# A hybrid encoder block on 8 cores: the opening pair made of both sequences' first groups, attention heads combined from PSUM, and the opening's loads and stages placed anew

## The chip, the cores and the metric

The kernel runs on the 8 NeuronCores of one Trainium2 chip. Each core takes 2 of the 16 sequences and the whole set of weights; the cores exchange nothing. The metric is the device time in microseconds of the slowest core, and the median of several runs.

## The reference, cut to what matters

Input and output are 16 sequences of 2048 tokens by 1024 floats. One layer:

```python
h = rms_norm(x);  proj = h @ w_in            # 1024 -> 2560: lru_x | lru_gate | q | k | v
lru_x = causal_dwconv(lru_x, width 4);  lru_h = rg_lru(lru_x)    # scan over time, 512 channels
out_a = gelu(lru_gate) * lru_h
p = softmax(q k^T / 8 + bias(T5) + block-causal mask)            # 4 heads, two maps per head
out_b = rms_norm((p1 - lam * p2) @ v)        # per head, value width 128
x = x + concat(out_a, out_b) @ w_out
h = rms_norm(x);  gate, val = split(h @ ffn_w_up)                # 2 x 3072
x = x + (gelu(causal_dwconv(gate, width 3)) * val) @ ffn_w_down
return rms_norm(x)
```

## The kernel before, in words

A core's 4096 tokens are cut into 8 groups of 512. `groups` (L642) lists them in the order of work: the four groups of sequence 0, then the four of sequence 1. Attention and the recurrence look back only, so group g of a sequence needs the keys, values and state of the groups before it; with g = 0 a head has 3 units of scores (two of 512 and one of 256 columns per map), with g = 1 it has 7, and 4 more for each further group.

The stages of a group are N (RMS norm and transposes), V, G, L, Q, K (the five 512-wide slabs of the input projection; L is the RG-LRU with its convolution, `lru` at L1005), B (attention, L1074), C (output projection, residual and second norm, L1181), and F or P (the MLP). The first two groups form a **pair** (`NP` = 2): they share each weight slab at the time when the weights come in as f32, are cast to bf16 and are written back to HBM (`load_slab`, `wslab`), and their residual rows stay in SBUF (`x0`). The MLP of the pair runs in thirds of its width (`stage_P`, L1250, with `plan` at L1415); later groups read the bf16 slabs back.

In B each head runs over its units: scores on TensorE (L1097), a bias on VectorE where the keys are near (L1114), exp on ScalarE (L1119), and the product with V on TensorE (L1130) into 8 regions of 129 columns in three PSUM banks, the last column being the sum of the weights. Three evictions (L901 on ScalarE, L903 on VectorE) then copy the regions to the SBUF tile `acp`, which frees the banks. Seven VectorE instructions follow: reciprocal (L1140), times -lambda (L1142), two products with the reciprocals (L1148, L1150), their sum (L1152), the square (L1153) and its row sum (L1155); then `rstd` (L849: an addition on VectorE at L850, a power on GpSimd at L853) and the product with it into `ob` (L1159).

No engine's order is written by hand. Each operation is a node with costs by engine and a priority; `schedule` (L162) places, node by node, the one that can start first by its estimated times, and among those that start together the one with the lowest priority number. That fixes the instruction order of every engine at build time, and on the chip each engine works in that order and waits on semaphores. The priorities come from `paced` (L1372), which spreads a stage over a stretch of "periods" from the tables `FR`, `PR`, `plan` and `e_` (L1387 to L1421). Where the estimate leaves TensorE idle, `_warm` (L306) puts in matmuls on a tile of zeros (L720). The four staging tiles for f32 weights lie in the key and value blocks of groups 2 and 3, so `claims` (L918) makes groups 2 and 3 wait until the staging is over.

At the start the SP queue issues the small parameters (L655), the f32 identity (L662, the first 128 columns of `stage`), then tiles of x (L651) and weights; the remaining 640 KB of `stage` come at L664. `ident` is cast on VectorE from the loaded one (L671), and the first transposes (L839) need it.

Of the kernel before, what the change touches and what calls it, by code (L numbers as in the profile page):

```python
# [9 lines left out]
F32 = mybir.dt.float32  # L10
BF16 = mybir.dt.bfloat16
# [10 lines left out]
SUBLN_EPS = 1e-5  # L22

# [56 lines left out]
class Node:  # L80
    __slots__ = ("i", "alts", "fn", "reads", "writes", "preds", "succs", "npred", "pri", "tab", "vts", "dma",
# [3 lines left out]
class Sched:  # L85
# [21 lines left out]
    def node(self, alts, fn, reads=(), writes=(), tab=None, dma=0, pri=None, tag="", after=(), behind=(), visit=None, soft=()):  # L107
        n = Node()
        n.i = len(self.nodes)
# [52 lines left out]
    def schedule(self, policy):  # L162
# [10 lines left out]
        dma_free = 0.0  # L173
# [35 lines left out]
        while placed < len(nodes):  # L209
            best = None  # L210
            for e in engs:
# [5 lines left out]
                for n in av:  # L217
# [50 lines left out]
            else:  # L268
                free[e] = t + hold
                n.fin = t + hold + TAIL[e]  # L270
# [178 lines left out]
def pack_params(inp):  # L449
# [31 lines left out]
    st.add("ident", np.eye(128, dtype=np.float32))  # L481
# [22 lines left out]
def build(nseq, S, pk_off, npar, nsmall, st_off, nst):  # L504
# [14 lines left out]
    wsl_d = nc.dram_tensor("wslab", [NSLAB, 128, 2048], BF16).ap()  # L519

    NPT, NSL = 3, 21

    with ExitStack() as st:
# [21 lines left out]
        lhalo = T("lhalo", [128, 4, 3], F32)  # L545
        lstate = T("lstate", [128, 4], F32)
        PT = T("PT", [128, NPT, 2, G], BF16)
        acp = T("acp", [128, 8, 129], F32)
# [3 lines left out]
        fhalo = T("fhalo", [128, 24, 2], F32)  # L552
# [10 lines left out]
        P_ob = Pool_("ob", 2)  # L563
        P_st = Pool_("stage", 4)
# [25 lines left out]
        for name, n in [("lam", 1), ("neglam", 1), ("e1", 1), ("e2", 1), ("s1", 1), ("s2", 1), ("cneg", 4), ("nba", 4),  # L590
                        ("nbx", 4), ("c2neg", 4), ("subg2", 1), ("mhalf", 1), ("rs", 8), ("rs2n", 4), ("sso", 4),
# [12 lines left out]
        b_stg2 = Buf()  # L604
        b_stage = [stg_vt, b_stg2]
        b_hT = [Buf() for t in range(NT)]
        b_hT2 = [Buf() for t in range(NT)]
        b_acp = Buf()
# [9 lines left out]
        b_lhaloc = [Buf() for c in range(4)]  # L618
        b_lstate = [Buf() for c in range(4)]
        b_fhalo = [Buf() for k in range(24)]  # L620
# [18 lines left out]

        S_.pri = 0  # L640
        ngrp = nseq * NG
        groups = [(sq, g) for sq in range(nseq) for g in range(NG)]  # L642
# [6 lines left out]
        def load_x(src_d, gi, t, cls, reads=(), **kw):  # L649
# [4 lines left out]

        node({"sp": 0.1}, lambda e: e.dma_start(out=prm[:, 0:nsmall], in_=par_d[:, 0:nsmall]), writes=[b_prm],  # L655
             dma=nsmall * 512, tag="prm", pri=-9)

        NP = 2
        x0 = [[load_x(x_d, 0, t, "XF", pri=-8 if t < 2 else -6.709) for t in range(NT)], []]
        stg_v = lambda: slot[:, stg_vt.s:stg_vt.s + 2, :].rearrange("p a b -> p (a b)")  # L660
        idn = Buf()
# [256 lines left out]
        def claims(gi):  # L918

            return {2: [b_stg], 3: [b_stg1]}.get(gi, [])  # L920
# [581 lines left out]
```

How the kernel before makes its waits and increments, by code:

```python
            def body(e):  # L403
                for fn, waits, sem, inc in self.prog[k]:
                    for s, v in waits:
                        e.wait_ge(self.sems[s], v)
                    if fn is not None:
                        fn(e).then_inc(self.sems[sem], inc)
```

The softmax here doesn't subtract the row's maximum and nothing guards it: scores larger than these inputs give would overflow.

## Time and profile before

| | us |
|---|---|
| median of 3 runs | 1764.8 (1762.7 to 1765.93) |
| span of the profiled execution, slowest core (core 0) | 1762.0 |
| span of core 1 in the same execution | 1754.9 |
| TensorE matmul busy on core 0, share of its span | 1694.3, 96% |
| VectorE, ScalarE, GpSimd busy on core 0 | 1168.4, 1072.0, 405.4 |

How to read it: the time of a run is that of its slowest core with some 3 us around the span. TensorE's busy time contains the matmuls on zeros, which do no work. Some of core 0's matmul records are missing from its trace (9445 matmuls beside 9628 weight loads), so the rows by stretch come from core 1, whose 9628 matmul records are whole.

### The profile page before, as it was taken

What the parts mean: (1) busy time and instruction counts of PE and PEld (TensorE: products, weight loads), DVE (VectorE), ACT (ScalarE), POOL (GpSimd) and SP (SyncE); (2) the same over time, 40 slices, a digit from 0 to 9 for tenths busy, and PEclk for the clock granted to TensorE, in tenths of its full rate; (3) what the DMA queues carried; (4) which work ended last, traced back from release to release, by engine and by line L of the source; (5) the groups of instructions that cost most, each with busy time, mean ns of one, the idle gap of its engine ahead of it and who ended that gap; (6) DMA issues with size and microseconds to landing.
All of it is one profiled execution on the core that took longest, in us unless ns stands there. A gap on an engine that the chain in (4) does not pass through costs nothing.

```text
span 1762.0 us, 31843 instructions; the slowest of 8 cores (1752.4 to 1762.0 us)
## 1 busy us (share of the span) xinstructions
PE 1694.3 (96%) x9445; PEld 803.9 (46%) x9628; DVE 1168.4 (66%) x2035; ACT 1072.0 (61%) x1419; POOL 405.4 (23%) x616
## 2 busy tenths in 40 slices
PE   8978899999999999999999999999999999999998
PEld 4434444444444444444444444444444444444443
DVE  3499857474687675757884597726877268764943
ACT  6778847356786586745854378444884458842721
POOL 2265413020331220113421042201322013210400
PEclk9999999999999999999999999999999999999999
DMA  9945299994447644559569545865458554447641
GB/s 275 293 142 170 69 304 290 290 289 144 147 155 239 191 153 137 190 161 268 187 207 266 149 172 203 230 203 171 147 171 223 189 169 147 161 140 218 223 175 72
DMA packets 165992, 340.53 MB, mean 193 GB/s; under 512 B 73664, under 2 KB 73920, under 8 KB 165696
## 3 DMA queue, kind: packets, MB, share of 16 engines
q1 hardware_dynamic: 165824, 338.49, 61.3%
q8 instruction: 81, 1.33, 0.3%
q14 instruction: 87, 0.71, 0.1%
HBM read 267.14 MB, written 55.57 MB: 183 GB/s over the span
## 4 chain that ended last, share of the span: by engine, by line
PE 83%; issue 5%; DVE 4%; DMA 4%; ACT 3%; POOL 1%; SPq 0%; DVEq 0%; ACTq 0%; POOLq 0%
PE pb L867 45%; PE pb L885 25%; PE pb L1130 6%; PE pb L1097 4%; DMA Va<-w_in 2%; PE pb L1328 1%; ACT PT L1119 1%; PE pb L720 1%; ACT raw L973 0%; DMA Va<-w_up 0%; DMA slot<-wslab 0%; DMA KT<-w_up 0%; DMA mixT<-ob 0%; ACT la L1031 0%; ACT thr L1031 0%
## 5 line engine op out<-in xcount | busy, mean ns | idle before, releaser
L867 PE MATMUL pb<-hT,slot 128*128 128x512 bf16 x3480 | 804.1, 380 | 18.1 <-issue 5.0
L867 PEld LDWEIGHTS pb<-hT,slot 128*128 128x128 bf16 x3584 | 336.0, 98 | 426.1 <-issue 52.3
L1119 ACT ACTIVATE PT<-pb,prm 128x1024 bf16<-128x1024 f32 (+1 forms) x288 | 305.7, 1063 | 153.3 <-PE pb L1097 74.0
L885 PE MATMUL pb<-slot,aT 128*128 128x512 bf16 x1494 | 345.0, 379 | 4.4 <-issue 1.4
L853 POOL TENSOR_TENSOR sm<-sm 128x1 f32<-128x1 f32 (+1 forms) x128 | 97.7, 765 | 633.4 <-DVE sm L850 633.1
L885 PEld LDWEIGHTS pb<-slot,aT 128*128 128x128 bf16 x1536 | 145.1, 98 | 178.7 <-issue 15.0
L1243 DVE TENSOR_TENSOR slot<-pb,slot 128x512 f32<-128x512 f32 x180 | 123.4, 688 | 142.5 <-PE pb L885 141.3
L1233 DVE TENSOR_TENSOR aT<-pb,aT 128x512 bf16<-128x512 f32 x192 | 130.6, 686 | 87.2 <-PE pb L867 82.4
L1130 PEld LDWEIGHTS pb<-Va,PT 128*128 128x128 bf16 x2176 | 142.5, 98 | 69.4 <-issue 20.6
L1130 PE MATMUL pb<-Va,PT 128*128 128x129 bf16 x2176 | 170.5, 221 | 2.0 <-ACT PT L1119 0.9
L990 DVE SCALAR_TENSOR_TENSOR facc<-raw,prm,facc 128x512 f32<-128x512 f32 x192 | 145.4, 761 | 32.1 <-ACT facc L984 22.7
L990 DVE SCALAR_TENSOR_TENSOR aT<-raw,prm,facc 128x512 bf16<-128x512 f32 x192 | 148.6, 778 | 7.3 <-DVE fhalo L976 0.3
L973 ACT ACTIVATE raw<-pb 128x512 f32<-128x512 f32 x164 | 97.7, 596 | 76.0 <-PE pb L867 51.4
L984 ACT ACTIVATE facc<-raw,prm 128x512 f32<-128x512 f32 x146 | 118.8, 814 | 27.6 <-DVE raw L973 9.8
L1114 DVE TENSOR_TENSOR pb<-pb,prm 128x512 f32<-128x512 f32 (+1 forms) x152 | 90.4, 595 | 49.4 <-PE pb L1097 47.9
L867 PE MATMUL pb<-aT,slot 128*128 128x512 bf16 x497 | 119.7, 384 | 3.4 <-DVE slot L904 2.2
L969 POOL COPY raw<-fhalo 128x2 f32<-128x2 f32 x168 | 68.0, 409 | 158.6 <-DVE aT L990 142.8
L885 PE MATMUL pb<-slot,mixT 128*128 128x512 bf16 x438 | 99.6, 382 | 2.6 <-DMA mixT<-ob 0.9
L1097 PE MATMUL pb<-qT,KT 64*128 64x512 bf16 (+3 forms) x576 | 98.3, 354 | 3.0 <-ACT PT L1119 2.7
L1224 ACT ACTIVATE aT<-aT 128x2048 bf16<-128x2048 bf16 x48 | 89.5, 1908 | 0.4 <-DVE aT L990 0.4
L814 ACT ACTIVATE hb<-slot 128x1024 bf16<-128x1024 f32 x38 | 40.0, 1053 | 69.5 <-DVE slot L1193 47.3
L1193 DVE TENSOR_TENSOR slot<-pb,slot 128x512 f32<-128x512 f32 x64 | 44.1, 689 | 55.1 <-PE pb L885 55.0
(138 smaller groups left out, 1662.9 us busy)
## 6 DMA issues: line engine op xcount, KB each, us to landing
slot<-wslab SPq DMA_DIRECT2D x326, 512.0 KB, 4.8
slot<-x SPq DMA_DIRECT2D x80, 512.0 KB, 7.1
wslab<-slot SPq DMA_DIRECT2D x50, 512.0 KB, 8.4
out<-slot SPq DMA_DIRECT2D x28, 512.0 KB, 5.5
x<-slot SPq DMA_DIRECT2D x24, 512.0 KB, 3.7
KT<-w_up SPq DMA_DIRECT2D x20, 512.0 KB, 6.4
Va<-w_up SPq DMA_DIRECT2D x20, 512.0 KB, 6.3
KT<-w_in SPq DMA_DIRECT2D x10, 512.0 KB, 10.6
```

The costliest lines, as they stand in the source:

```text
L853: op("pool", 1.0, lambda e: e.tensor_tensor(out=smv(rsn, 0, n), in0=smv(ssn, 0, n), in1=smv("mhalf").to_broadcast([128, n]), op=ALU.pow), ...
L867: last = e.matmul(bank(p), lhsT=w[:, kk, cc * 128:(cc + 1) * 128], rhs=src[:, hf * 4 + kk, :], start=(hf == 0 and kk == 0), stop=(hf == 1 ...
L885: last = e.matmul(bank(p), lhsT=src[:, k0 + hf * 4 + kk, t * 128:(t + 1) * 128], rhs=w[:, kk, :], start=(hf == 0 and kk == 0), stop=(hf == ...
L973: return e.activation(out=o, in_=bank(p), func=AF.Copy) if e is nc.scalar else e.tensor_copy(out=o, in_=bank(p))
L984: return e.activation(out=o, in_=i, func=AF.Identity, scale=w_ap[:, n:n + 1], bias=b_ap)
L990: nd = op("dve", dve_us(512, ptr=1), lambda e, k=k, last=last: e.scalar_tensor_tensor(out=out if last else tile[:, v.s, :], in0=raw[:, r_. ...
L1097: last = e.matmul(psum[:, s.s + c, n0:n0 + n], lhsT=KT[c * 64:(c + 1) * 64, j // NT, h, (j % NT) * 128:(j % NT + 1) * 128], rhs=q_()[c * 6 ...
L1114: op("dve", dve_us(2 * wn), lambda e, s=s, wn=wn, n0=n0, bias_ap=bias_ap: e.tensor_tensor(out=psum[:, s.s:s.s + 2, n0:n0 + wn], in0=psum[: ...
L1119: op("act", act_us(2 * N, ptr=1), lambda e, s=s, pt=pt, N=N, h=h: e.activation(out=PT[:, pt.s, :, 0:N], in_=psum[:, s.s:s.s + 2, 0:N], fun ...
L1130: last = e.matmul(psum[:, acc[ab].s, off:off + 129], lhsT=PT[:, pt.s, c, q0:q0 + 128], rhs=Va[:, j, h, 0:129], start=(j == 0 and rr % 3 == 0),
L1233: op("dve", dve_us(512), lambda e, p=p, a=a: e.tensor_tensor(out=aT[:, a, :], in0=bank(p), in1=aT[:, a, :], op=ALU.mult), reads=[p], write ...
L1243: return e.tensor_tensor(out=xs, in0=bank(p), in1=xs, op=ALU.add)
```

## The change

1. **Order of groups.** `groups` becomes (0,0), (1,0), (0,1), (0,2), (0,3), (1,1), (1,2), (1,3), written here as (sequence, group). The pair is now the first group of each sequence. Halos and states of the convolutions and the scan get one copy per sequence. Keys and values of (1,0) are kept in block 1, stored to a new HBM tensor `kv` (`save_v` and the end of `stage_K`, 0.5 MB each) and brought back into block 0 before group (1,1) (`bring_kv`). `claims` moves from groups 2 and 3 to 3 and 4.
2. **Heads combined from PSUM.** The 8 regions are laid out in three neighbouring banks held as one piece (class `acc`, first bank 2). The three evictions are gone. After reciprocal and -lambda, four 128-wide ScalarE instructions scale the second map from PSUM into the new `acp` tile, four 128-wide VectorE instructions multiply the first map from PSUM and add, four more square with an accumulated sum, and one 512-wide instruction applies `rstd` as before.
3. **Identity on chip.** A memset and an affine_select on GpSimd instead of load and cast.
4. **Opening loads.** The first x tile is issued first, then the small parameters, x tiles 1 to 3, the first weights, and only then `stage` in one piece.
5. **Estimates and places.** Costs of GpSimd operations are lowered; VectorE operations marked `lk` wait, in the estimate, for GpSimd to be free and keep it waiting until they end; the addition in `rstd` may go to GpSimd. All place tables have new numbers, and thirds 2 and 3 of `plan` change their order.

```diff
+PLAN = {
+    "PR": {"N0": (-6.075, -6.633), "N1": (-6.336, -5.832), "V": (-6.445, -6.616, 0.491), "G": (-6.224, -6.595, 0.644),
+           "L0": (-6.074, -5.643), "Q": (-5.988, -5.895, 0.207), "K": (-6.015, -5.702, 0.777), "L1": (-4.943, -3.721),
+           "B0": (-6.001, -5.45), "B1": (-4.798, -2.917), "C": (-4.561, -2.744)},
+    "P": [(-4.283, -3.284), (-3.436, -2.186), (0.46, 0.735), (-0.01, 0.432), (0.855, 2.235)],
+    "WB": 0.712,
+    "S": [-7.967, -6.709, -6.709, -6.3, -5.846],
+}
...
-        PR.update({'N0': (-6.391, -6.385), 'N1': (-6.336, -5.832), 'V': (-6.603, -6.546, 0.322), 'G': (-6.231, -6.583, 0.677), 'L0': (-6.098, -5.643), 'Q': (-5.988, -5.895, 0.497), 'K': (-6.015, -5.702, 0.672), 'L1': (-4.943, -3.721), 'B0': (-6.001, -5.45), 'B1': (-4.686, -3.5), 'C': (-4.573, -2.551)})
-        plan = [(0, {0: 0}, 'F', -4.391, -3.392), (1, {0: 0}, 'F', -3.299, -2.384), (0, {1: 8}, 'A', 0.124, 0.653), (1, {1: 0}, 'A', 0.66, 1.007), (2, {0: 8, 1: 0}, 'F', 0.855, 2.116)]
...
+                    if e == "dve" and n.lk:
+                        t = tt = max(t, free["pool"])
+                    elif e == "pool" and t < locked:
+                        t = tt = locked
...
-        groups = [(sq, g) for sq in range(nseq) for g in range(NG)]
+        groups = [(sq, 0) for sq in range(nseq)] + [(sq, g) for sq in range(nseq) for g in range(1, NG)]
+        kblock = lambda gi, i: gi if gi < NP else i
...
-        x0 = [[load_x(x_d, 0, t, "XF", pri=-8 if t < 2 else -6.709) for t in range(NT)], []]
-        node({"sp": 0.1}, lambda e: e.dma_start(out=stg_v()[:, 0:128], in_=stg_d[:, 0:128]), writes=[stg_vt, idn],
-             dma=128 * 512, tag="stg", pri=-8.5)
+        x0 = [[load_x(x_d, 0, t, "XF", pri=-20 if t == 0 else SP_[t - 1]) for t in range(NT)], []]
+        node({"sp": 0.1}, lambda e: e.dma_start(out=stg_v()[:, 0:nst], in_=stg_d[:, 0:nst]), writes=[stg_vt, b_stg2],
+             dma=nst * 512, tag="stg", pri=SP_[3], behind=[x0[0][0].ld])
+        op("pool", 0.2, lambda e: e.memset(ident[:], 1.0), writes=[b_ident], pri=-30)
+        op("pool", 0.5, lambda e: e.affine_select(out=ident[:], in_=ident[:], pattern=[[-1, 128]], compare_op=ALU.is_equal,
+                                                  fill=0.0, base=0, channel_multiplier=1), writes=[b_ident], pri=-29)
...
+        def bring_kv(gi):
+            node({"sp": 0.1}, lambda e: e.dma_start(out=KT[:, 0, :, :].rearrange("p h q -> p (h q)"), in_=kv_d[0]),
+                 reads=[b_kvd[0]], writes=[b_KT[h][0] for h in range(4)], dma=524288, tag="kv")
+            node({"sp": 0.1}, lambda e: e.dma_start(out=Va[:, 0:NT, :, 0:128], in_=kv_d[1].rearrange("p (t h c) -> p t h c", t=NT, h=4)),
+                 reads=[b_kvd[1]], writes=b_V[0:NT], dma=524288, tag="kv")
...
-                for ab, r0, nr in ((0, 0, 3), (1, 3, 3), (2, 6, 2)):
-                    evac(acc[ab], acp[:, r0:r0 + nr, :], b_acp, n=nr * 129,
-                D_(dve_us(512), lambda e: e.tensor_tensor(out=O1, in0=O1, in1=bc(smv("rs", 0, 4)), op=ALU.mult),
-                D_(dve_us(512), lambda e: e.tensor_tensor(out=O2, in0=O2, in1=bc(smv("rs2n")), op=ALU.mult),
-                D_(dve_us(512), lambda e: e.tensor_tensor(out=O1, in0=O1, in1=O2, op=ALU.add), [], [b_acp])
-                D_(dve_us(512), lambda e: e.scalar_tensor_tensor(out=O2, in0=O1, scalar=1.0 / 128.0, in1=O1, op0=ALU.mult,
-                D_(dve_us(512), lambda e: e.tensor_reduce(out=smv("sso"), in_=O2, axis=AX.X, op=ALU.add),
+                def scaled(e):
+                    for il in range(NT):
+                        last = e.activation(out=dd(il), in_=val(il, 1), func=AF.Identity, scale=rs(1)[:, il:il + 1])
+                    return last
+                def both(e):
+                    for il in range(NT):
+                        last = e.scalar_tensor_tensor(out=dd(il), in0=val(il, 0), scalar=rs(0)[:, il:il + 1], in1=dd(il),
+                                                      op0=ALU.mult, op1=ALU.add)
+                    return last
+                def squares(e):
+                    for il in range(NT):
+                        last = e.scalar_tensor_tensor(out=ob[:, o.s, il, :], in0=dd(il), scalar=1.0 / 128.0, in1=dd(il),
+                                                      op0=ALU.mult, op1=ALU.mult, accum_out=smv("sso", il, il + 1))
+                    return last
```

## Rows read from the trace of the kernel before

**Rows 1.** The page's heading line.
```profile
span 1762.0 us, 31843 instructions; the slowest of 8 cores (1752.4 to 1762.0 us)
```

**Rows 2.** Core 1 by stretch: length, busy by engine (instructions), clock, DMA share, GB/s.
```profile
80.00:200.00 120.00, 99.83 (x695) 49.08 (x693) 113.54 (x203) 100.39 (x152) 63.71 (x58) 0.97 0.40 127
0.00:240.00 240.00, 214.06 (x1273) 101.36 (x1274) 170.56 (x316) 178.56 (x265) 93.59 (x97) 0.99 0.67 208
240.00:1720.00 1480.00, 1467.29 (x8228) 690.04 (x8227) 984.88 (x1694) 887.47 (x1138) 307.38 (x516) 1.00 0.62 195
```

**Rows 3.** Core 1, the same stretches, L720 alone (matmuls on zeros; PE, PEld).
```profile
80.00:200.00 120.00, 17.08 (x63) 5.38 (x63) 0.97 0.40 127
0.00:240.00 240.00, 39.88 (x147) 13.89 (x147) 0.99 0.67 208
240.00:1720.00 1480.00, 11.68 (x41) 3.93 (x41) 1.00 0.62 195
```

**Rows 4.** Core 1, timeline of the start: SP, ScalarE, TensorE (start, length, what).
```profile
1.98 1.84 SPq L651 DMA_DIRECT2D slot<-x  x4
...
6.40 0.43 SPq L664 DMA_DIRECT2D slot<-stage  x1
...
7.77 1.06 ACT L814 ACTIVATE hb<-slot 128x1024 bf16<-128x1024 f32 x1 [2.81 <-DMA slot<-x]
...
19.48 3.62 PE L885 MATMUL pb<-slot,hT 128*128 128x512 bf16 x16
```

**Rows 5.** Core 1, DMA issues in 0 to 40 us: size, us to landing.
```profile
slot<-stage SPq DMA_DIRECT2D x1, 640.0 KB, 12.8
...
slot<-stage SPq DMA_DIRECT2D x1, 64.0 KB, 3.2
```

**Rows 6.** Core 1, 80 to 200 us: instructions on acp (DVE, ACT), then L1142 (DVE).
```profile
80.00:200.00 120.00, 36.47 (x55) 6.62 (x15) 0.97 0.40 127
...
80.00:200.00 120.00, 3.08 (x7) 0.97 0.40 127
```

**Rows 7.** Core 1, VectorE groups by shape, 80 to 200 us (busy, mean ns, idle before).
```profile
L1114 DVE TENSOR_TENSOR pb<-pb,prm 128x512 f32<-128x512 f32 x22 | 15.1, 688 | 0.6 <-PE pb L1097 0.6
L1150 DVE TENSOR_TENSOR acp<-acp,sm 128x512 f32<-128x512 f32 x7 | 6.2, 884 | 0.0
...
L1114 DVE TENSOR_TENSOR pb<-pb,prm 128x256 f32<-128x256 f32 x12 | 5.0, 421 | 0.0
L1148 DVE TENSOR_TENSOR acp<-acp,sm 128x512 f32<-128x512 f32 x7 | 4.8, 681 | 0.0
```

**Rows 8.** Core 1, VectorE groups of the whole span: a 64-wide product, an accumulator read.
```profile
L816 DVE DVE_READ_ACCUMULATOR hb<-slot 128x1 f32 x26 | 2.1, 82 | 0.0
...
L677 DVE TENSOR_TENSOR sm<-slot 128x64 f32<-128x64 f32 x2 | 0.4, 222 | 0.1
```

**Rows 9.** Core 1, ScalarE groups by shape, 80 to 200 us.
```profile
L1119 ACT ACTIVATE PT<-pb,prm 128x1024 bf16<-128x1024 f32 x32 | 35.5, 1117 | 3.6 <-DVE pb L1114 1.9 <-PE pb L1130 1.0 <-PE pb L1097 0.7
...
L1031 ACT ACTIVATE thr<-pb,sm 128x512 f32<-128x512 f32 x7 | 4.8, 685 | 2.3 <-DVE acp L1148 1.7 <-PE pb L1024 0.6
...
L901 ACT ACTIVATE acp<-pb 128x258 f32<-128x258 f32 x7 | 2.7, 385 | 0.4 <-DVE acp L903 0.2
```

**Rows 10.** Core 1, chain that ended last, 150 to 200 us: one unit's TensorE time.
```profile
156.36 0.45 PE pb L1130 x8
...
161.27 0.32 PE pb L1097 x2
```

**Rows 11.** Core 1, timeline across a head's end, 1457 to 1462 us.
```profile
1457.94 0.39 PE L1130 MATMUL pb<-Va,PT 128*128 128x129 bf16 x4
...
1461.50 0.20 DVE L1140 RECIPROCAL sm<-acp 128x8 f32<-128x8 f32 x1
...
1461.65 0.56 PE L1130 MATMUL pb<-Va,PT 128*128 128x129 bf16 x7
```

**Rows 12.** Core 1, timeline of TensorE: the first gate matmuls of group 0's MLP.
```profile
188.30 1.89 PE L867 MATMUL pb<-hT,slot 128*128 128x512 bf16 x8
```

More of the change, by code:

```diff
@@ L104, in __init__, with node @@
         self.grp = 0
-    def node(self, alts, fn, reads=(), writes=(), tab=None, dma=0, pri=None, tag="", after=(), behind=(), visit=None, soft=()):
+    def node(self, alts, fn, reads=(), writes=(), tab=None, dma=0, pri=None, tag="", after=(), behind=(), visit=None, soft=(), lk=False):
         n = Node()
+        n.lk = lk
         n.i = len(self.nodes)
@@ L269, in schedule @@
                 free[e] = t + hold
+                if e == "dve" and n.lk:
+                    locked = free[e]
                 n.fin = t + hold + TAIL[e]
@@ L563, in build @@
         P_ob = Pool_("ob", 2)
+        P_dd = Pool_("acp", 1)
         P_st = Pool_("stage", 4)
@@ L952, in stage_K @@
                     evac(p, KT[:, g, h, :], b_KT[h][g], stg=stg)
+                if 0 < gi < NP:
+                    node({"sp": 0.1}, lambda e, g=g: e.dma_start(out=kv_d[0], in_=KT[:, g, :, :].rearrange("p h q -> p (h q)")),
+                         reads=[b_KT[h][g] for h in range(4)], writes=[b_kvd[0]], dma=524288, tag="kv")
         def stage_V(*gis):
@@ new lines, in stage_B, with pieces_of @@
+            d = g * NT
+            last_j = {0: d, 1: d + 1, 2: d + 2, 3: d + 2}
+            where = lambda il, c: divmod(383 * il + 129 * c, 512)
+            first = [None]
+            kb = [kblock(gi, i) for i in range(g + 1)]
+            vt = lambda j: kb[j // NT] * NT + j % NT
+            def pieces_of(js):
+                pieces, n0 = [], 0
+                for j in js:
+                    i0 = max(0, j - d)
+                    pieces.append((j, i0, n0, (NT - i0) * 128))
+                    n0 += (NT - i0) * 128
+                return pieces, n0
@@ new lines, in scores, with qk @@
+            def scores(h, js):
+                s = VT(P_ps, n=2, cls="qk2" if gi in (0, 1) else "qk")
+                pieces, N = pieces_of(js)
+                def qk(e):
+                    for j, i0, n0, n in pieces:
+                        for c in range(2):
+                            last = e.matmul(psum[:, s.s + c, n0:n0 + n],
+                                            lhsT=KT[c * 64:(c + 1) * 64, kb[j // NT], h, (j % NT) * 128:(j % NT + 1) * 128],
+                                            rhs=q_()[c * 64:(c + 1) * 64, h, i0 * 128:G], start=True, stop=True)
+                    return last
+                nq = op("pe", 0.24 + N / 2400.0, qk, reads=[b_KT[h][kb[js[0] // NT]], b_qT[h]], writes=[s], tag="qk")
+                if h == 3 and js[0] == 0:
+                    first[0] = nq
+                return s, pieces, N
@@ L1414, in build @@
         units = None
-        plan = [(0, {0: 0}, 'F', -4.391, -3.392), (1, {0: 0}, 'F', -3.299, -2.384), (0, {1: 8}, 'A', 0.124, 0.653), (1, {1: 0}, 'A', 0.66, 1.007), (2, {0: 8, 1: 0}, 'F', 0.855, 2.116)]
-        for third, at, line, f0, f1 in plan:
+        for third, at, line, k in THIRDS:
+            f0, f1 = PLAN["P"][k]
             u1 = units
```

265 lines of the change are left out of this document (124 added, 141 removed), and 4 rows, old and new, of the table PLAN.

## The prediction

> **What bounds the kernel now.** I read the heading line first: the slowest core spans 1762.0 us and the eight lie within 10 us [rows 1], so there is no straggler to repair; the median, 1764.8, is 2.8 us above that span. The next view is the table by stretch with TensorE's busy time, beside the same table for the matmuls on zeros, which are busy but do nothing. From 240 to 1720 us TensorE is idle for 1480 - 1467.3 = 12.7 us and on zeros for 11.7 us: 24 us lost in 1480, 1.6% [rows 2, 3]. In the first 240 us it is idle for 25.9 us and on zeros for 39.9: 66 us lost, 27% [rows 2, 3]. So TensorE bounds the later part, where any matmul added costs its full length, and something else bounds the opening.
>
> The opening has two losses. Up to 19.5 us TensorE has nothing but zeros and transposes, because the first projection waits for x and for the first weights [rows 4]. From 80 to 200 us it loses 120 - 99.8 + 17.1 = 37 us, while VectorE is busy for 113.5 of the 120 (95%) and ScalarE for 100.4 (84%) [rows 2, 3]: here two RG-LRUs, two attentions, the residuals and the norms run on VectorE and ScalarE, and group 0's MLP, the work that could fill TensorE, starts only at 188 us [rows 12]. The reader is to see that VectorE sets this stretch, and that work taken from VectorE in it is worth its length, but only as far as it carries little TensorE work away with it.
>
> **Opening loads and identity.** Before, the small parameters, the f32 identity (64 KB, 3.2 us to landing) and then x are issued; x goes out at 1.98 us and its first square starts at 7.77 [rows 4, 5]. Now x is first, so up to about a microsecond earlier (it had two issues ahead of it in its 1.98). The 640 KB of `stage` went out at 6.40, between the first weights [rows 4, 5]; it now goes behind them. The opening moves 208 GB/s at a DMA share of 0.67 [rows 2], 310 at a full share: 0.70 MB are 2.3 to 3.4 us. Both shift the start of the same chain, and the weights' staging tiles, not the bytes, may hold it: 0 at worst, 4.4 together at best. I take **-2.6**. Two GpSimd instructions for the identity cost nothing: the norm they must beat has not begun at 7.77 [rows 4]; without that cover it is about a microsecond. What `stage` feeds (the gates' weights, lambda) is used after the projections, dozens of us later.
>
> **The new pair.** Group 1 has 3 units a head instead of 7, so 16 units of 2 x 512 scores leave the opening. A unit costs ScalarE 1.117 us [rows 9]: 17.9 us. On TensorE it costs 0.32 for the scores and 0.45 for the product with V [rows 10]: 12.3 us. VectorE loses one 256-wide bias a head, 0.42 [rows 7]: 1.7 us. None of this disappears: the units come back in a later group. There ScalarE and VectorE are busy for 60% and 67% [rows 2] and hide their share, but TensorE is not hidden: **+12.3 us** after 240.
>
> **Combining a head from PSUM.** Before, the instructions on `acp` take 36.5 us of VectorE and L1142 another 3.1, over seven heads: 5.65 us a head; ScalarE's evictions 6.62 over seven, 0.95 [rows 6]. After: a reciprocal and a multiplication as they were (0.2 and 0.44, as in L1142's row [rows 6]), one 512-wide product at 0.74 (taken like L1148 to L1150, 0.68 to 0.88 [rows 7]), and eight 128-wide VectorE instructions that no row shows. Their bounds are the 64-wide product, 0.222 [rows 8], and the 256-wide bias from PSUM, 0.421 [rows 7]; 128 columns with a scalar per partition lie nearer to the middle and upwards, and I take 0.35 for the four from PSUM and 0.29 + 0.08 for the four squares, each followed by an accumulator read of 0.082 [rows 8]. That is 1.40 + 1.48 = 2.88, 4.26 in all: 1.4 us saved a head (0.6 to 2.2 by the bounds), 11.2 us for the opening's eight (5 to 17). ScalarE's four scalings from PSUM lie below 0.385 (258 columns) and below 0.685 (512 with a scalar) [rows 9]; I take 0.36, 1.44 a head, so ScalarE gains 0.5 a head, 4 us in the opening.
>
> The Trainium skill speaks against such slicing: "VectorE: DVE Perf Modes", the section on the TRN2 errata, says that every SBUF-sourced instruction pays a fixed latency, so that many small tiles pay it many times, and advises tiles of at least 512 elements. Its formulas, 120 + N cycles from PSUM and 58 + N from SBUF at 0.96 GHz, would make the eight instructions, with reads of 0.082, an estimated 2.1 us, so by them the opening would gain another 6 us; no row here shows either at 128 columns.
>
> So the stretch from 80 to 200 us loses 11.2 + 1.7 = 12.9 us of VectorE and 17.9 - 4 = 13.9 of ScalarE, and gets shorter by about the former. With 12.3 us of TensorE moved to where it counts, pair and combination together give **-0.6** (+6 to -7 by the bounds on the combination). The pair alone is nearly neutral: its attention units kept TensorE as busy as ScalarE.
>
> **Places.** L1 keeps its numbers and C0's hardly move, but B1 now runs to -2.917 while the first third of group 0's MLP ends at -3.284; before, B1 ended at -3.5. The later two of its heads can fall beside the MLP, where VectorE and ScalarE have room. Each such head takes 4.26 for the combination and 3 x 0.688 + 0.421 for its biases off VectorE in the tight stretch [rows 7], 6.7 us; two give 13.5, less their six units on TensorE at 0.77: **-8.9**. Since the planner places what can start first and looks at priorities only then, it may be 0; the other end is -13.5.
>
> **Later groups.** There the combination's saving is hidden. What is new is that the three accumulator banks stay taken until the last PSUM reader is done. Before, the reciprocal, which follows the three evictions, begins 3.2 us after a head's last product ended, and the next head's first product 0.15 us after that [rows 11]. Now the release also waits for the multiplication, 1.44 of ScalarE and 1.40 of VectorE, less the evictions: some 2 to 3 us more a head, for 24 heads. Queued behind a product that waits are all the matmuls of TensorE; the cover is the MLP matmuls that the plan puts between two heads. I take **+1** (0 to +10). The four `kv` transfers move 2 MB, 10 us of the core's 195 GB/s [rows 2] beside 1480 us of other work; their risk is order: `bring_kv` waits on SP for the last readers of block 0, and weight slabs are queued behind it there. I take 0 (to +3), as block 0 is needed again only a stage later. Moving `claims` frees group 2 from the staging and binds group 4: 0.
>
> **Sum.** -2.6 - 0.6 - 8.9 + 1 = -11.1: a span of 1750.9 on the profiled execution, with 2.8 around it **1754 us**. Its own range is 1741 to 1766.
>
> **The rivals.** *The new estimates repair the order itself.* In the opening the same 512-wide product takes 0.884 at L1150 and 0.681 at L1148 [rows 7]; the plan before gave them one cost, and in a fixed order each overrun is passed to whoever waits. With VectorE and GpSimd kept apart in the plan a third of the opening's 66 us might go: 22 us, 1743. Against it: GpSimd's costs were lowered too, which can err the other way. The Trainium skill, "SBUF — State Buffer", section "Who interferes with whom", states that a VectorE instruction with two SBUF inputs and a GpSimd one that reads SBUF exclude one another, while one with a single SBUF input does not; by that rule the new multiply-add is exempt and the squares are not.
>
> *The places bring nothing:* the places' term is 0, -2.6 - 0.6 + 1 = -2.2, 1763. For it: the rule of first start. Against it: the late start at 188 us [rows 12] shows how much of group 1's work now runs ahead of the MLP.
>
> *The banks are released too late (slower):* a product that comes while ScalarE or VectorE is deep in other work stalls TensorE. If 24 heads wait 0.75 us each beyond the forecast, 18 us, the time is 1772; it decides from 0.5 us a head, where the gain is gone. For it: ScalarE and VectorE have to be free in turn, and in an in-order queue neither is at once. Against it: the planner knows the banks' owner and puts other matmuls first.
>
> **How the numbers follow.** I give the forecast 0.55, the repaired order 0.17, the places that bring nothing 0.14, the late banks 0.14. About 0.2% (3.5 us) is what a measurement can tell from no change: faster below 1761.3, slower above 1768.3. The forecast is faster in 0.50 of its 0.55, the same in 0.03, slower in 0.02; the second is faster; of the third 0.11 is the same and 0.03 faster; of the fourth all is slower. Faster 0.70, same 0.14, slower 0.16. The range 1736 to 1770 leaves out the far part of the repaired order and half of the late banks.
>
> **What would show it.** In the profile of the changed kernel: the first projection near 17 us; a combination near 4.3 us of VectorE a head; 128-wide instructions near 0.35; the first gate matmul of group 0 well before 188 us; TensorE's loss in the first 240 us down from 66 to some 54; the loss from 240 to 1720 still near 24. I am wrong if that last loss grows by more than 10 us with waits of L1130 on VectorE, or if VectorE is still at 95% and the first gate matmul as late.

## The result, and the profile after

The changed kernel takes 1745.3 us against 1764.8: a ratio of 0.9892 (95%: 0.9876 to 0.9908), 19.5 us or 1.1% faster. All comparisons below are of undisturbed executions (three of the changed kernel's five, median 1744.7); a second, slower state of the others left experiment e7 a single time and no interval, and the profiled execution of e8 only cores 0, 1, 6 and 7.

The heading line of the page after, which answers to [rows 1]:

```profile
span 1742.5 us, 31867 instructions; the slowest of 8 cores (1733.8 to 1742.5 us)
```

Core 1 of the changed kernel by stretch, columns as in [rows 2]; the second fence has its matmuls on zeros (L742 now) for the latter two stretches and answers to [rows 3]:

```profile
80.00:200.00 120.00, 95.63 (x565) 45.86 (x563) 105.58 (x274) 105.84 (x173) 39.90 (x45) 0.91 0.67 208
0.00:240.00 240.00, 213.12 (x1171) 100.65 (x1172) 169.31 (x402) 193.63 (x308) 64.52 (x90) 0.96 0.80 249
240.00:1720.00 1480.00, 1475.47 (x8380) 696.53 (x8378) 953.70 (x1929) 884.04 (x1167) 238.12 (x417) 1.00 0.62 190
```

```profile
0.00:240.00 240.00, 25.63 (x88) 8.98 (x88) 0.96 0.80 249
240.00:1720.00 1480.00, 12.99 (x51) 4.62 (x51) 1.00 0.62 190
```

A stretch less TensorE's busy time is its idle time: a wait. The matmuls on zeros fill the holes that the order has by design. The sum of the two I call the **loss**. In the first 240 us it fell from 65.8 to 26.9 + 25.6 = 52.5 us; the holes shrank, the waits did not. Later the waits fell from 12.7 to 4.5 and the zeros rose a little, from 11.7 to 13.0.

From 80 to 200 us VectorE fell from 113.5 to 105.6 busy, ScalarE rose from 100.4 to 105.8. The two are level now. One core tells little of a few us, so the comparisons below take the median of the six cores whose matmul records are whole (four for e8), and end at 1700 us. So read, the opening's loss went from 66.5 to 54.2 (-12.3) and the later loss from 25.0 to 19.2 (-5.8): 18.1 of the 19.5 us. Of the opening's part 5.2 us fall before 80 us (24.7 to 19.5), 4.1 from 80 to 200 (37.9 to 33.8) and 3.9 after that (4.3 to 0.4); medians of parts do not add up exactly.

The start and the first gate matmul (timeline of core 1; answers to [rows 4] and [rows 12]): x goes out 0.9 us earlier, its first square starts 1.1 earlier, the first projection 2.5 earlier, group 0's MLP 28 us earlier.

```profile
1.07 0.40 SPq L675 DMA_DIRECT2D slot<-x  x1
...
6.69 1.06 ACT L836 ACTIVATE hb<-slot 128x1024 bf16<-128x1024 f32 x1
...
17.01 1.24 PE L907 MATMUL pb<-slot,hT 128*128 128x512 bf16 x5
...
160.51 1.89 PE L889 MATMUL pb<-hT,slot 128*128 128x512 bf16 x8 [0.17 <-ACT aT L923]
```

The new instructions of a combination, groups by shape over core 1's whole span (busy, mean ns), then VectorE and ScalarE on the tile `acp` by stretch (DVE, ACT), and the first stretch of the same table before, which answer to [rows 6 to 8]:

```profile
L1200 DVE SCALAR_TENSOR_TENSOR acp<-pb,sm,acp 128x128 f32<-128x128 f32 x128 | 35.8, 341 | 4.1 <-ACT acp L1193 3.9
L1209 DVE SCALAR_TENSOR_TENSOR ob<-acp 128x128 bf16<-128x128 f32 x128 | 30.8, 294 | 1.0 <-DVE acp L1200 0.7
L1209 DVE DVE_READ_ACCUMULATOR ob<-acp 128x1 f32 x128 | 10.2, 80 | 0.0
L1193 ACT ACTIVATE acp<-pb,sm 128x128 f32<-128x128 f32 x128 | 36.4, 371 | 9.0 <-DVE sm L1188 7.5 <-DVE lstate L1094 1.6
```

```profile
0.00:240.00 240.00, 22.77 (x104) 9.06 (x32) 0.96 0.80 249
240.00:1720.00 1480.00, 66.28 (x312) 27.32 (x96) 1.00 0.62 190
```

```profile
0.00:240.00 240.00, 40.99 (x62) 7.98 (x18) 0.99 0.67 208
```

Each instruction's mean is what was forecast (0.35, 0.29 + 0.08), but the windows count time once, and instructions of a run overlap. For the opening's eight heads the tile takes 22.77 / 8 = 2.85 us of VectorE a head, the last product of 0.69 included: 2.15 for the eight with their reads, not 2.88. With the small instructions beside it (3.30 us at L1142 before; 1.58 at L1186 and 2.65 at L1188 after) the opening's eight heads take 44.3 us of VectorE before and 27.0 after: 17.3 saved. A head's boundary shows it (timeline of core 1; answers to [rows 11]):

```profile
882.67 0.39 PE L1170 MATMUL pb<-Va,PT 128*128 128x129 bf16 x4
...
883.55 0.20 DVE L1186 RECIPROCAL sm<-pb 128x8 f32<-128x8 f32 x1
883.85 0.23 DVE L1188 TENSOR_SCALAR sm<-sm 128x4 f32<-128x4 f32 x1
884.55 1.14 ACT L1193 ACTIVATE acp<-pb,sm 128x128 f32<-128x128 f32 x4
...
885.93 1.11 DVE L1200 SCALAR_TENSOR_TENSOR acp<-pb,sm,acp 128x128 f32<-128x128 f32 x4
...
887.21 1.07 PE L1170 MATMUL pb<-Va,PT 128*128 128x129 bf16 x16
887.22 0.29 DVE L1209 SCALAR_TENSOR_TENSOR ob<-acp 128x128 bf16<-128x128 f32 x1 [0.18 <-DVE acp L1200]
887.44 0.08 DVE L1209 DVE_READ_ACCUMULATOR ob<-acp 128x1 f32 x1
887.44 0.28 DVE L1209 SCALAR_TENSOR_TENSOR ob<-acp 128x128 bf16<-128x128 f32 x1
```

Four products of 341 ns take 1.11 us, and the squares start every 0.22. The banks are held from the last product's end at 883.06 to the end of their last reader at 887.04: 3.98 us. At the boundary of [rows 11] the trace has 3.07, but that is one of the longest before. Another one of core 1 before has 1.78 (1070.74 to 1072.52):

```profile
1070.35 0.39 PE L1130 MATMUL pb<-Va,PT 128*128 128x129 bf16 x4
...
1071.43 1.09 DVE L903 COPY acp<-pb 128x387 f32<-128x387 f32 x2 [0.83 <-ACT acp L901]
```

Over core 1's 24 later heads the median hold is 1.79 us before and 3.97 after, 2.2 more. It costs almost nothing: of TensorE's waits from 240 to 1700 us (core 1; total, times, longest) one alone is on the combination.

```profile
PE pb L1135 <- ACT PT L1160: 1.0, 4, 0.4
...
PE pb L1170 <- DVE acp L1200: 0.2, 1, 0.2
```

### The profile page after: what moved, and what is told of

Same layout as the page of the kernel before. It is cut to its first block, busy times and chain, and to the rows that moved or that the text cites. A ratio compares the mean times of both kernels' runs of the same rounds, so it can differ in the third digit from the quotient of the medians.

```text
span 1742.5 us, 31867 instructions; the slowest of 8 cores (1733.8 to 1742.5 us)
## 1 busy us (share of the span) xinstructions
PE 1700.5 (98%) x9579; PEld 801.3 (46%) x9579; DVE 1130.9 (65%) x2341; ACT 1079.2 (62%) x1478; POOL 304.9 (18%) x508
## 4 chain that ended last, share of the span: by engine, by line
PE 91%; DMA 3%; ACT 2%; issue 2%; DVE 1%; POOL 1%; SPq 0%; DVEq 0%; ACTq 0%; POOLq 0%
PE pb L889 50%; PE pb L907 26%; PE pb L1170 7%; PE pb L1135 5%; PE pb L1387 1%; PE pb L742 1%; DMA KT<-w_out 1%; ACT PT L1160 1%; DMA slot<-wslab 1%; DMA slot<-x 1%; DMA Va<-w_down 0%; PE pb L1060 0%; PE pb L1062 0%; DMA Va<-w_up 0%; POOL sm L875 0%
## 5 line engine op out<-in xcount | busy, mean ns | idle before, releaser
L889 PE MATMUL pb<-hT,slot 128*128 128x512 bf16 x3584 | 825.2, 380 | 7.2 <-DVE aT L1294 3.7
L907 PE MATMUL pb<-slot,aT 128*128 128x512 bf16 x1536 | 352.4, 379 | 1.0 <-ACT qT L923 0.8
L1304 DVE TENSOR_TENSOR slot<-pb,slot 128x512 f32<-128x512 f32 x180 | 123.1, 688 | 137.4 <-PE pb L907 136.7
L1026 DVE SCALAR_TENSOR_TENSOR aT<-raw,prm,facc 128x512 bf16<-128x512 f32 x192 | 144.5, 759 | 4.0 <-DVE facc L1026 0.5
L1009 ACT ACTIVATE raw<-pb 128x512 f32<-128x512 f32 x143 | 84.4, 595 | 82.6 <-PE pb L889 54.3
L1020 ACT ACTIVATE facc<-raw,prm 128x512 f32<-128x512 f32 x141 | 113.6, 812 | 24.4 <-DVE raw L1009 12.9
L1155 DVE TENSOR_TENSOR pb<-pb,prm 128x512 f32<-128x512 f32 (+1 forms) x152 | 90.2, 595 | 36.6 <-PE pb L1135 34.5
L1135 PE MATMUL pb<-qT,KT 64*128 64x512 bf16 (+3 forms) x608 | 104.7, 356 | 6.9 <-ACT PT L1160 6.5
L1009 DVE COPY raw<-pb 128x512 f32<-128x512 f32 x81 | 55.4, 688 | 45.0 <-PE pb L889 42.8
L847 ACT ACTIVATE hb<-slot,sm 128x1024 bf16<-128x1024 f32 x45 | 51.5, 1146 | 51.8 <-POOL sm L875 47.9
```

Of the source, the lines that this page charges most:

```text
L889: last = e.matmul(bank(p), lhsT=w[:, kk, cc * 128:(cc + 1) * 128], rhs=src[:, hf * 4 + kk, :], start=(hf == 0 and kk == 0), stop=(hf == 1 ...
L907: last = e.matmul(bank(p), lhsT=src[:, k0 + hf * 4 + kk, t * 128:(t + 1) * 128], rhs=w[:, kk, :], start=(hf == 0 and kk == 0), stop=(hf == ...
L1009: return e.activation(out=o, in_=bank(p), func=AF.Copy) if e is nc.scalar else e.tensor_copy(out=o, in_=bank(p))
L1020: return e.activation(out=o, in_=i, func=AF.Identity, scale=w_ap[:, n:n + 1], bias=b_ap)
L1026: nd = op("dve", dve_us(512, ptr=1), lambda e, k=k, last=last: e.scalar_tensor_tensor(out=out if last else tile[:, v.s, :], in0=raw[:, r_. ...
L1135: last = e.matmul(psum[:, s.s + c, n0:n0 + n], lhsT=KT[c * 64:(c + 1) * 64, kb[j // NT], h, (j % NT) * 128:(j % NT + 1) * 128], rhs=q_()[c ...
```

## The experiments

Three theories stood after this. **Estimates**: the new estimates give an order that the chip can keep, since TensorE's later waits fell from 13.5 to 6.2 us while the work for it hardly changed (the prediction's first rival). **Work**: what counts is the opening's lighter work. **Tables**: the place numbers, which were chosen for the kernel as it is, carry the gain. All loss figures are medians over cores as above; e5 to e8, e11 and e12 have places of their own, found by 1500 random changes judged by the planner's own estimate (for e8 and e11 without the loads, which keep their priorities of before).

| kernel | median us | ratio to before (95%) | loss 0 to 240 | loss 240 to 1700, waits + zeros |
|---|---|---|---|---|
| before | 1764.8 | 1 | 66.5 | 13.5 + 11.5 |
| after | 1745.3 | 0.9892 (0.9876 to 0.9908) | 54.2 | 6.2 + 13.0 |
| e1 old estimates | 1766 | 1.0016 (1.0006 to 1.0026) | 65.4 | 14.9 + 12.5 |
| e2 old places | 1800 | 1.0212 (1.0195 to 1.0229) | 68.2 | 12.1 + 46.0 |
| e3 old pair | 1775 | 1.0061 (1.0046 to 1.0076) | 58.9 | 12.8 + 31.8 |
| e4 old loads | 1785 | 1.0116 (1.0096 to 1.0136) | 68.0 | 7.5 + 36.9 |
| e5 after, new tables | 1739.2 | 0.9861 (0.9836 to 0.9885) | 54.1 | 7.3 + 4.8 |
| e6 old pair, new tables | 1744.3 | 0.9892 (0.9869 to 0.9914) | 54.0 | 7.0 + 10.9 |
| e7 old combination, new tables | 1757.4 (one) | none | 66.8 | 11.4 + 4.7 |
| e8 all old work, new tables | 1756.8 | 0.9965 (0.9953 to 0.9977) | 67.7 | 11.9 + 9.6 |
| e9 combination padded | 1784.2 | 1.0114 (1.0096 to 1.0131) | 61.7 | 33.0 + 13.0 |
| e10 old issue order | 1750.0 | 0.9918 (0.9899 to 0.9937) | 57.5 | 5.7 + 13.0 |
| e11 old loads, new tables | 1750.6 | 0.9922 (0.9898 to 0.9946) | 62.9 | 7.4 + 5.5 |
| e12 old estimates, new tables | 1737.7 | 0.9852 (0.9828 to 0.9876) | 53.4 | 7.9 + 5.7 |

**e1 to e4: one part undone, the changed kernel's tables kept.**

```diff
# e1: GpSimd's costs of before, VectorE and GpSimd not kept apart, rstd's addition on VectorE alone
-        n.lk = lk
+        n.lk = False
# e2: FR, PR, plan, E, WB and S of before
# e3
-        groups = [(sq, 0) for sq in range(nseq)] + [(sq, g) for sq in range(nseq) for g in range(1, NG)]
+        groups = [(sq, g) for sq in range(nseq) for g in range(NG)]
# e4: the loads and the loaded identity of before, with their priorities
```

> The changed kernel, planned with the old estimates: GpSimd's old costs, no rule that keeps VectorE and GpSimd apart, the addition of rstd on VectorE alone. Everything computed and all place tables stay. The changed kernel lost 13 us less than the old one in the first 240 us and 7 us less after it; my prediction had 12 and -1. Theory 1 (the later gain comes from the estimates, which give an order that TensorE waits for less): the time goes back by 7 us or more, to 1752 or above, with TensorE's loss after 240 us back near 24 us. Rival (the later gain comes from the place tables, or from the lighter combination): 1745 within 3 us, loss after 240 us still near 17 us.

> The changed kernel with the old place tables (stages, thirds of the pair's MLP, write-backs, opening loads' numbers). By my prediction the places are worth 8.9 us, all in the opening: about 1754, with the first gate matmul of group 0 later than 160 us and TensorE's loss in the first 240 us up from 52 to about 61 us. Rival (the places also carry the later gain): 1761, with the loss after 240 us near 24 us. Rival (the places bring nothing, since the planner takes what can start first): 1745 within 3 us.

> The changed kernel with the old order of groups: the pair is (0,0) and (0,1) again, without the store of keys and values and its return. By my prediction the pair alone is nearly neutral (13 us of ScalarE in the opening against 12.3 us of TensorE after it): 1745 within 4 us, the opening's loss unchanged near 52 us, VectorE and ScalarE busier in 80 to 200 us. Rival (taking 16 attention units out of the opening is what let group 0's MLP start at 160 us): 1755 or more, the MLP's start back towards 180 us.

> The changed kernel with the old opening loads: small parameters and f32 identity first, x after them, the rest of stage ahead of the last first weights. By my prediction 2.6 us are lost: 1748, with the first projection matmul back near 19.5 us instead of 17.0. Rival (the weights' staging tiles hold the start, or the opening catches up later): 1745 within 1 us although the first projection is late. Rival (other stages shift with it): more than 5 us.

Each part undone loses more than the whole change gained, 21 to 56 us. e1 spoke for the estimates: the waits are back at 14.9. But in e2 to e4 most of the loss is in zeros after 240 us, in e4 too, where the loads of the opening have long been done. Core 1 of e3, the matmuls on zeros after 240 us (12.99 us with the change whole):

```profile
240.00:1720.00 1480.00, 31.82 (x126) 11.38 (x126) 1.00 0.61 189
```

Those holes are in the order itself: what fits is that tables chosen for other work space its stages wrongly. So these four measure a misfit, and say little on their parts. The parts had to be undone with places of their own.

**e5: the changed kernel with tables found in that way, the control of those that follow.**

> The changed kernel with nothing altered but its place tables, which were searched further for the earliest planned end (1500 small random steps). It is the control for the three kernels beside it, whose tables got the same search. If a plan made with the new estimates holds on the chip, it ends below the changed kernel's 1745: about 1736, with TensorE's waits (idle, not zeros) from 240 to 1700 us no more than the 4.5 us of the changed kernel. Rival (a better plan on paper is lost again to waits that it doesn't know): 1745 within 3 us, the idle time up by what the matmuls on zeros lose.

It beats the changed kernel by 5.5 us, 0.3%; the waits stay at 7.3 us where no more than 4.5 were expected. The opening's loss is the same; the later one falls by 7. The same work under two tables, then, differs by about 6 us, and a difference that small between two kernels with tables of their own shows nothing. That is one pair of tables; how far more of them would scatter was not measured.

**e6, e7, e11: one part undone (edits of e3 and e4; for e7 the `stage_B` and the `acp` of before, with two small tiles cut to make room for it), each with new tables.**

> The old pair, (0,0) and (0,1), with everything else of the change, and with place tables searched anew for it by the same 1500 steps. With the changed kernel's tables the old pair took 1775. If the 29 us of that run were the tables' misfit and the pair is nearly neutral, as predicted: within 4 us of the control beside it. Rival (the pair is a main part of the gain): 10 us or more above the control.

> The old combination (three evictions to SBUF, seven VectorE instructions) with everything else of the change, and tables searched anew by the same 1500 steps; a start-up scratch shares a tile so that the larger copy fits. By my prediction the combination is worth 11 us of VectorE in the opening and nothing later, so 5 to 11 us above the control. Rival (VectorE doesn't set the opening once the MLP starts early): within 3 us of the control.

> The old opening loads and the loaded identity, with everything else of the change, and tables searched anew by the same 1500 steps as the control's. With the changed kernel's tables the old loads took 1782. If that was the tables' misfit: 2 to 6 us above the control's 1739. Rival (the loads carry a larger part): 10 us or more above it.

Against e5, by the ratios: the old pair costs 5.5 us, none of it in the opening (54.0 to 54.1); it is within what tables alone can do. The old loads cost 11, 9 of them in the opening. The old combination costs 18 by the medians, where 5 to 11 were expected, 13 of them in the opening and 4 later; e7's is a single time, but the slowest core of each die of four, 1751.6 to 1755.6 us on the five usable dies of e7 and 1731.3 to 1739.0 on the eight of e5, puts them 17 apart. Core 1 of e7 by stretch, and its matmuls on zeros:

```profile
0.00:240.00 240.00, 211.87 (x1167) 98.03 (x1168) 169.90 (x326) 186.15 (x280) 66.28 (x84) 0.96 0.77 237
240.00:1720.00 1480.00, 1468.33 (x8340) 693.23 (x8338) 1001.84 (x1806) 895.96 (x1137) 229.20 (x405) 1.00 0.61 192
```

```profile
0.00:240.00 240.00, 38.36 (x143) 13.56 (x143) 0.96 0.77 237
240.00:1720.00 1480.00, 4.70 (x18) 1.76 (x18) 1.00 0.61 192
```

The whole loss of the opening before is back, 28.1 + 38.4 = 66.5 us on this core. But not all of it can be the combination's, as the loss by stretch shows (medians as above):

| kernel | 0 to 80 | 80 to 200 | 200 to 240 |
|---|---|---|---|
| before | 24.7 | 37.9 | 4.3 |
| after | 19.5 | 33.8 | 0.4 |
| e5 after, new tables | 19.3 | 33.9 | 0.5 |
| e6 old pair, new tables | 23.6 | 27.6 | 2.9 |
| e7 old combination, new tables | 26.2 | 36.6 | 4.3 |
| e9 combination padded | 19.9 | 40.5 | 0.9 |
| e10 old issue order | 22.7 | 33.8 | 0.7 |
| e11 old loads, new tables | 23.1 | 34.0 | 5.6 |

By 80 us e7 has lost 6.9 us more than e5, and its first combination begins only at 83.64 us (core 1). Its new tables differ in more than was asked: `stage` goes out among the first weights again, where e5 has it behind them (timeline of core 1, e7 and then e5; in e6 it goes out at 4.03). The rows behind them are core 1's first 80 us in e7 and e5, each with its matmuls on zeros:

```profile
3.94 0.78 SPq L697 DMA_DIRECT2D slot<-stage  x1
```

```profile
8.53 0.64 SPq L696 DMA_DIRECT2D slot<-stage  x1
```

```profile
0.00:80.00 80.00, 75.57 (x392) 34.70 (x393) 33.62 (x73) 53.95 (x82) 16.45 (x29) 1.00 0.95 290
0.00:80.00 80.00, 21.58 (x82) 8.16 (x82) 1.00 0.95 290
```

```profile
0.00:80.00 80.00, 76.99 (x406) 35.83 (x407) 36.33 (x78) 59.08 (x92) 15.36 (x29) 1.00 0.96 294
0.00:80.00 80.00, 17.06 (x60) 6.23 (x60) 1.00 0.96 294
```

In the eight kernels with `stage` among or ahead of the first weights the loss up to 80 us is 22.7 to 26.2; in the six with it behind them it is 19.3 to 19.9, and 22.3 and 23.3 in the two that are planned by the old estimates. So e6 and e7 undo a part of the loads as well. What is left to e7's combination in the opening are the 6.4 us after 80 us (34.4 to 40.8, medians), and e11 has 5.4 more than e5 there with the new combination (39.8). So e7 alone does not give the combination's price.

**e8: all three parts old, with the new estimates and tables of its own.**

> The kernel before in all that it executes (old pair, old combination, old identity and opening loads), planned with the new estimates and with tables searched anew by the same 1500 steps. Theory (the estimates and the tables that fit them are the larger part of the gain): about 1750, that is most of the 19.5 us without any of the three changes of the work. Rival (the changed work is the gain): 1760 or more. Either way the waits (idle) from 240 to 1700 us should be near 5 us, not the 12.7 of the kernel before.

It is 6 us (4 to 8) faster than before, with no gain in the opening (67.7): tables and estimates by themselves. Its later waits are 11.9 us, where about 5 were expected if the estimates carried the gain. It is as slow as e7, which has `stage` early too; what the new loads bring beside the old combination was therefore not measured. The three singly make 5.5 + 11 + 18 = 34 us, together they make 18 (e8 against e5): e6 and e7 count a part of the loads again, 4.3 and 6.9 us up to 80 us, and the rest was not separated.

**e9: four products of 384 columns added on VectorE behind each head's squares, written to a scratch tile that nobody reads; the order of all else kept.**

```diff
+                    if n.fn.__name__ == "squares":
+                        for _ in range(2):
+                            o.append((policy["pad"](n.reads[0]), t))
...
+                for k in range(2):
+                    last = e.tensor_tensor(out=extra[:, k, :], in0=i, in1=i, op=ALU.mult)
```

> The changed kernel with its plan, tables and order untouched, and after the squares of each head four products of 384 columns on VectorE into a scratch tile that nobody reads: about 2.2 us more of VectorE a head, what the old combination took beside the new one. If VectorE's time in the combination is what the opening gained by (13 us between the kernels with the old and the new combination whose tables got the same search), the time goes up by 10 to 18 us for the eight heads of the opening, TensorE's loss in the first 240 us from 52 to 62 or more, and little is added later. Rival (the gain came from the evictions' place on ScalarE and from the release of the banks, not from VectorE's time): less than 5 us.

The price of VectorE's time, measured by itself. Core 1, the added line, and its busy time in the opening and later:

```profile
L767 DVE TENSOR_TENSOR extra<-acp 128x384 bf16<-128x384 f32 x128 | 66.5, 561 | 3.7 <-DVE extra L767 0.5
```

```profile
0.00:240.00 240.00, 16.40 (x32) 0.94 0.77 238
240.00:1720.00 1480.00, 50.07 (x96) 1.00 0.62 189
```

16.4 us added in the opening, about the 17.3 that the new combination saves there, raise its loss by 7.5, nearly all of it from 80 to 200 us; 50.1 added later raise the later loss by 26.8: 0.46 and 0.53 us lost per us of VectorE. The expectation was 10 to 18 us with little later; it was 39. In an order that stays as it is, the later groups hide no more than half, with VectorE 64% busy there before the padding. It is the price of this place in a fixed order: the padding also holds up the rest of its head, and an order made anew could hide more.

**e10: small parameters and `stage` put back to where they were issued, all other orders kept.**

```diff
+        o.insert(0, par)
+        o.insert(next(k for k, x in enumerate(o) if x[0].tag == "ldw"), stg)
```

> The changed kernel with its plan and order untouched but for SP's first issues: the small parameters go ahead of the first x tile, and the 640 KB of stage ahead of the first weights, as before; the identity is still made on chip. By my prediction the loads are worth 2.6 us: 1748, the first projection matmul at 19 to 20 us instead of 17.0, and TensorE's loss in the first 80 us up by as much. Rival (the delay is caught up by 80 us, where the weights' arrival sets the pace anyway): within 1 us of 1745.

5 us slower than the change (the two intervals just overlap). The loss to 80 us rises by 3.2, and the first projection starts at 21.45 instead of 17.01 (timeline of core 1). That is later than the 19 to 20 expected and than the 19.48 before, so it costs somewhat more than the old loads themselves:

```profile
1.06 0.40 SPq L688 DMA_DIRECT2D prm<-params  x1
...
3.39 0.84 SPq L691 DMA_DIRECT2D slot<-stage  x1
...
21.45 1.89 PE L914 MATMUL pb<-slot,hT 128*128 128x512 bf16 x8 [0.34 <-ACT slot L811]
```

**e12: the changed work, ordered by the estimates of before, with tables of its own.** The edit of e1, and new tables: e1 made fair.

> The changed kernel's whole work, but ordered by the estimates of the kernel before (GpSimd's old, higher costs, VectorE and GpSimd not kept apart, the rstd addition on VectorE alone), with its places searched anew for these estimates, as long as the control's were for the new ones (control: 1739.2 us). Theory, that the new estimates make an order that the chip can keep: TensorE's unplanned waits come back, idle 240 to 1700 at 11 to 16 us (control 7.3, median of the cores with whole records), idle 0 to 240 at 30 or more (27.0), time 1746 to 1760. Rival, that the estimates bring nothing and the places all: idle within 2 us of 7.3 in the later part, time 1735 to 1744.

The rival holds: 1737.7 us, no slower than e5, waits of 7.9 against 7.3. Core 1 by stretch:

```profile
0.00:240.00 240.00, 213.29 (x1176) 99.09 (x1177) 170.58 (x397) 183.81 (x281) 101.50 (x108) 0.97 0.77 241
240.00:1720.00 1480.00, 1470.53 (x8352) 694.93 (x8351) 958.65 (x1863) 893.59 (x1185) 266.58 (x477) 1.00 0.62 191
```

GpSimd is again busy for 101.5 us in the opening. The theory of the estimates, which I held after e1, falls: e1's waits came from tables chosen under other estimates. e12 is also the fastest of all, though not to be told from e5: 0.9852 of the kernel before, 26 us.

## Why the prediction came out as it did

The forecast was -11.1 us, the result is -19.5, inside the range. Its sum for the opening, -2.6 - 0.6 - 8.9 = -12.1, meets the measured -12.3, but by luck, since terms that are off cancel. It put 9.5 us (0.6 + 8.9) into the stretch from 80 to 200 us; 4.1 came there, 5.2 before it and 3.9 after it. Its later term, +1, had the wrong sign.

- **Loads, -2.6 (0 to -4.4): near in size, but not by the first projection.** That came at 17.01, as forecast, but it does not measure the loads: on core 1 the new ones start it at 15.27 in e7 and 20.47 in e6, the old ones at 17.49 in e11. Up to 80 us the old loads cost 3.2 us in e10 and 3.8 in e11. In all e10 puts the order of issue at 5 us and e11, with new tables, at 11; of the latter 5 are lost from 200 to 240 us, and what they are was not separated: tables can differ by as much.
- **Combination, VectorE 4.26 us a head: mis-sized.** Each instruction's length was right; adding the lengths was wrong, since they overlap. Measured in the opening: 0.20 + 0.33 for the small ones, 2.15, 0.69, so 3.4 a head. Over eight heads 17.3 us are saved, not 11.2: the forecast's upper bound. e9 puts them at some 8 us of the opening. The Trainium skill's formulas, "VectorE: DVE Perf Modes", section on the TRN2 errata, gave an estimated 2.1 for the eight, and the trace agrees with 2.15: here the page was nearer than my reading of neighbouring rows. Its advice against small tiles did not decide, since five 512-wide passes went. ScalarE's four scalings take 9.06 / 8 = 1.13 a head, not 1.44.
- **The new pair, 12.3 us of TensorE moved to where it counts: wrong.** By the forecast's terms the old pair should be better by 12.3 - 1.7 = 10.6 us; e6 is 5.5 us worse. The forecast's other sentence, that the pair alone is nearly neutral, does not follow from these terms and came nearer. The opening's loss is the same with either pair: the units moved out of it leave room that other matmuls fill, so a us moved is not a us lost. With `stage` early, e6 loses 4.3 us more up to 80 us and 3.8 less from there to 240 (30.6 to 34.4, medians), so the old pair may have some of the advantage that the terms give it; whether the pair gains anything stays open.
- **Places, -8.9: its mechanism not seen.** The reason was the MLP's start beside the second pair member's heads. The start did come earlier, 160.5 us. But in e8 it is at 174.1 against [rows 12], and the opening's loss is no smaller; in e6 it is at 175.6, and the loss is that of e5, whose start is at 162.8. With the old work, then, the rival that places bring nothing in the opening was right; for the new work no run parts the two (e2 loses 68.2 there, with a table that does not fit). What tables do bring lies in the later groups in e5 (5.5 us) and, as far as the two losses show it (25.0 to 21.5), in e8.
- **Later groups, +1 for banks held longer, the rest hidden: wrong sign.** The hold grew by 2.2 us a head, as forecast (2 to 3), yet one wait of 0.2 us is all that core 1 shows: TensorE's other work between two heads covers it, and the rival of the late banks falls. That the saving is hidden does not hold in a fixed order, where e9 prices it at half a us per us of VectorE; with the order made anew e7 gives 4 us, less than tables alone move that loss. Measured for the whole change: -5.8. The transfers of `kv` cost nothing that a wait of TensorE shows.
- **The repaired order, 1743:** the time is near, the cause is not. With the old estimates the same work takes 1737.7 (e12). The Trainium skill's rule in "SBUF — State Buffer", "Who interferes with whom", may well hold on the chip; planning by it gave nothing that could be measured here.
- **What bounds the opening from 80 us on** was read rightly, VectorE: e9 adds time to it alone, and the loss follows at 0.46 us per us. Over the first 240 us it is as busy as before (170.6 and 169.3 us on core 1), since other work filled what was saved. Relieving it hands part of the bound to ScalarE, which the forecast did not say. Core 1 from 80 to 120 us, before and then after:

```profile
80.00:120.00 40.00, 32.28 (x210) 14.51 (x208) 36.67 (x63) 33.55 (x55) 23.98 (x18) 0.96 0.51 163
```

```profile
80.00:120.00 40.00, 26.75 (x172) 13.59 (x170) 35.77 (x101) 38.44 (x66) 15.29 (x13) 0.81 0.85 260
```

ScalarE goes from 33.6 to 38.4 of 40 us, and TensorE does less than before there; what is gained between 80 and 200 us is gained after 120.

So, as far as shown: in an order that is kept, giving VectorE back about what the combination saved costs the opening 7.5 us (e9), and putting the loads back costs it 3.3 (e10), together 10.8 of its 12.3. With the order made anew the two are not parted cleanly: e7 has 12.7 and e11 8.8, but e7 undoes a part of the loads too. The opening's gain needs neither the new pair (e6) nor the new estimates (e12). Of the later 5.8, all within the 7 us by which tables alone move that loss, no part is settled.

## What to carry to other kernels

Where an order is made by a planner with numbers chosen for one kernel, a part undone under those numbers measures the misfit: choose them anew for each variant, with equal effort, measure the scatter with a control, and look whether the new numbers have undone another part on the way. Price several short instructions of one engine by the time from the first start to the last end, not by the sum of their lengths. A bound taken off one engine is worth its length only until the next engine is level; look at that engine's share in the same stretch before summing.

## What the runs showed of the hardware

A VectorE instruction of 128 columns from PSUM shows 341 ns, yet four in a row take 1.11 us: they start every (1.11 - 0.34) / 3 = 0.26 us. ScalarE's four scalings of 371 ns take 1.14, by the same reckoning also one every 0.26. From 80 to 120 us the mean granted clock was 0.81 in the changed kernel (0.96 before), a mix of the 2.4 and the 1.2 GHz level. Stretches of 5 us of core 1 after, columns as in [rows 2]:

```profile
90.00:95.00 5.00, 2.67 (x12) 0.87 (x10) 5.00 (x15) 4.91 (x11) 2.66 (x2) 0.96 0.84 301
95.00:100.00 5.00, 5.00 (x33) 3.33 (x32) 3.44 (x14) 4.32 (x8) 2.73 (x3) 0.70 0.88 257
100.00:105.00 5.00, 2.57 (x18) 0.91 (x16) 3.95 (x9) 4.97 (x10) 2.71 (x2) 0.98 0.97 320
105.00:110.00 5.00, 3.96 (x28) 2.45 (x27) 5.00 (x19) 4.61 (x8) 1.93 (x2) 0.68 0.73 223
110.00:115.00 5.00, 0.70 (x5) 0.35 (x4) 3.86 (x7) 4.78 (x10) 2.55 (x3) 0.66 0.98 308
115.00:120.00 5.00, 2.93 (x17) 1.51 (x18) 4.66 (x16) 4.91 (x10) 0.00 (x0) 0.50 0.64 218
```

The stretch after one with TensorE busy for 2.67 us has 0.70, the one after a fully busy stretch has 0.98. From 105 us on the clock is at 0.50 to 0.68, with TensorE busy for 0.7 to 4.0 of each 5 us and ScalarE for 4.6 to 4.9. Of TensorE's 13.2 us of idle time from 80 to 120 us the trace puts 9.8 on ScalarE. The product with V shows what it costs, by mean ns on core 1, before and after:

```profile
L1130 PE MATMUL pb<-Va,PT 128*128 128x129 bf16 x80 | 6.2, 220 | 0.0
```

```profile
L1170 PE MATMUL pb<-Va,PT 128*128 128x129 bf16 x71 | 7.5, 282 | 0.0
```

Each is shown 62 ns longer. But these lengths overlap too: by busy time it is 7.5 / 71 = 0.106 us instead of 6.2 / 80 = 0.078, some 2 us for the 71. Since ScalarE, not TensorE, is the one that is full in this stretch, how much of it reaches the end was not measured.
